# An MoE trunk layer on one core: weights of an expert in one row, in a ring of 24 slabs with two halves

## What is computed

```python
logits = (t @ w_router + b_router)            # 32 experts
top_val, top_idx = lax.top_k(logits, TOP_K)   # 4 for each token
gates = softmax(top_val)
# for each expert e, on the tokens that chose it:
up = xb @ w_up[e] + b_up[e]                   # 1024 -> 2048
glu, lin = up[:, :1024], up[:, 1024:]
glu = minimum(glu, 7.0); lin = clip(lin, -7.0, 7.0)
act = glu * sigmoid(1.702 * glu) * (lin + 1)
y = act @ w_down[e] + b_down[e]               # 1024 -> 1024
```

## Time and profile before

| what | value |
|---|---|
| median of 3 runs | 1153.88 us (1153.6 to 1154.08) |
| profiled execution, span | 1152.1 us |
| PE busy | 1130.9 us (98%) |
| VectorE, ScalarE, GpSimd busy | 358.9, 221.7, 85.2 us |
| read from HBM | 436.18 MB, 379 GB/s over the span |
| DMA queue q1 (the loads) | 89.4% of 16 engines' span |
| granted TensorE clock | 0.997 |

### The profile page before, as it was taken

The page is one execution under the profiler, slowest core; times in us unless marked ns, Lnnn a source line. Parts: engine busy times, 40 slices in busy tenths (PEclk is TensorE's granted clock), DMA queues, the critical chain, the costliest instruction groups (busy, mean ns, idle before and its releaser), DMA issues.

```text
span 1152.1 us, 16029 instructions
## 1 busy us (share of the span) xinstructions
PE 1130.9 (98%) x5376; PEld 502.2 (44%) x5377; DVE 358.9 (31%) x933; ACT 221.7 (19%) x429; POOL 85.2 (7%) x206
## 2 busy tenths in 40 slices
PE   9999999999999999999999999999999999999999
PEld 6785487653333333333333333333333333333333
DVE  6898413232222222222222222222222222222223
ACT  5321213121111121111111111111111111111113
POOL 2990000000000000000000000000000000000000
PEclk9999999999999999999999999999999999999999
DMA  9464336389999999999999999999999999999995
GB/s 364 188 272 176 146 146 282 156 347 429 429 435 431 427 433 433 427 432 433 396 421 437 437 422 433 437 432 423 437 437 424 431 437 433 424 426 429 424 426 244
DMA packets 28821, 437.76 MB, mean 380 GB/s; under 512 B 4017, under 2 KB 4657, under 8 KB 12017
## 3 DMA queue, kind: packets, MB, share of 16 engines
q1 hardware_dynamic: 27920, 436.10, 89.4%
q10 hardware_dynamic: 864, 1.14, 0.3%
HBM read 436.18 MB, written 1.05 MB: 379 GB/s over the span
## 4 chain that ended last, share of the span: by engine, by line
PE 77%; DMA 20%; SPq 1%; ACT 1%; issue 0%; DVE 0%; ACTq 0%; DVEq 0%
PE bank L1813 28%; DMA ring<-in_w_up_dram 20%; PE bank L1858 16%; PE total L1773 4%; PE bank L1760 4%; PE bank L1452 2%; PE bank L1471 2%; PE bank L1866 2%; PE bank L1683 2%; PE bank L1462 2%; PE bank L1767 1%; PE bank L1617 1%; PE total L1617 1%; DMA ring<-in_w_in_dram 1%; PE bank L1911 1%; PE bank L1576 1%
## 5 line engine op out<-in xcount | busy, mean ns | idle before, releaser
L1813 PE MATMUL bank<-ring,buf_m 128*64 128x512 f32 (+1 forms) x2192 | 465.2, 581 | 13.4 <-DMA ring<-in_w_up_dram 13.3
L1813 PEld LDWEIGHTS bank<-ring,buf_m 128*64 128x64 f32 x2192 | 156.9, 138 | 316.1 <-issue 286.4
L1858 PE MATMUL bank<-ring,buf_m 128*64 128x512 f32 x1056 | 239.9, 595 | 0.0
L1343 DVE COPY buf_f<-bank 128x512 f32<-128x512 f32 x32 | 22.1, 692 | 448.6 <-PE bank L1813 448.6
L1858 PEld LDWEIGHTS bank<-ring,buf_m 128*64 128x64 f32 x1056 | 72.8, 136 | 136.5 <-issue 126.5
L888 ACT ACTIVATE buf_m<-buf_f 128x256 f32<-128x256 f32 x32 | 13.3, 416 | 333.1 <-DVE buf_f L1353 333.1
L1773 PE MATMUL total<-buf_m,wr_sb 64*128 64x512 f32 x272 | 67.6, 615 | 1.6 <-ACT buf_m L897 0.8
L656 POOL TENSOR_TENSOR buf_v<-table,buf_v 128x4 f32<-128x4 f32 x33 | 6.6, 201 | 775.6 <-DVE buf_v L1331 775.3
L1760 PE MATMUL bank<-buf_k,buf_v 128*64 128x512 f32 x264 | 63.9, 605 | 0.0
L1349 DVE TENSOR_TENSOR buf_f<-bank,buf_v 128x512 f32<-128x512 f32 x64 | 44.0, 687 | 57.7 <-PE bank L1866 57.7
L897 ACT ACTIVATE buf_m<-bank,buf_v 128x512 f32<-128x512 f32 x32 | 22.0, 687 | 194.1 <-PE bank L1858 194.1
(11 more groups left out here) (389 smaller groups left out, 884.4 us busy)
## 6 DMA issues: line engine op xcount, KB each, us to landing
ring<-in_w_up_dram SPq DMA_DIRECT2D x48, 4096.0 KB, 30.0
ring<-in_w_down_dram SPq DMA_DIRECT2D x24, 4096.0 KB, 30.4
ring<-in_w_up_dram SPq DMA_DIRECT2D x29, 2048.0 KB, 15.3
ring<-in_w_down_dram SPq DMA_DIRECT2D x13, 2048.0 KB, 38.2
ring<-in_w_down_dram SPq DMA_DIRECT2D x6, 1024.0 KB, 10.8
ring<-in_w_up_dram SPq DMA_DIRECT2D x6, 1024.0 KB, 38.5
ring<-in_w_in_dram SPq DMA_DIRECT2D x4, 1024.0 KB, 17.2
ring<-in_w_xkv_dram SPq DMA_DIRECT2D x2, 2048.0 KB, 27.4
```

The lines of the kernel that those rows point to most:

```text
L1813: ins = t_.matmul(banks[bank][h * 64:(h + 1) * 64, c0:c1], xg[:, k, :], w[:, :, k % 4, h, :], start=first, stop=last)
L1858: ins = t_.matmul(banks[2][h * 64:(h + 1) * 64, :], actT[:, f, :], group(slot_of(at))[:, lo + h * BANK:lo + (h + 1) * BANK], start=f == 0, ...
```

## The change

The ring grows to 24 slabs in two halves of twelve; expert e always takes half e % 2. The last two slabs take the place of `buf_v` (slab 22) and `buf_x` (slab 23). w_up and w_down of an expert are joined on the host to one row of twelve slabs per partition (`w_expert`). Experts 4 to 7 are still loaded in three transfers of four slabs, experts 8 to 27 in two of six. The first of them waits for three of the four up groups of expert e-2, the second for the end of its down products. Second, w_xo is loaded in two parts: the second right behind w_out, into slabs 20 and 21, the first behind xq3. The loads that fill the ring first come in another order. g_final goes into slab 0 and is loaded while expert 30 runs, behind all up weights of expert 31 and w_down's first half. Third, small buffers move: the router's constants are written by GpSimd behind xo3, sig and actT lie in U's space. The wait on "late" in VectorE's last section is as before; the diff does not touch it. What PE computes in an expert is the same.

```diff
-RING, LOADS, CYCLE = 20 // GROUP, 12 // GROUP, 5
-TURNS = (E - 2) // CYCLE - 1
-WIDE_FROM, WIDE_TO = 4, 28
+SLABS = 12
+WIDE_FROM, SIX_FROM, SIX_TO = 4, 8, 28
...
-        ring = sb("ring", 20 * SLAB)
+        ring = sb("ring", 2 * SLABS * SLAB)
...
-        wxo_sb = slab(4, 4).rearrange("p (k n) -> p k n", k=KT)
-        buf_x = sb("buf_x", TT * D)
+        wxo_sb = slab(18, 4).rearrange("p (k n) -> p k n", k=KT)
+        buf_v = slab(22)
+        buf_x = slab(23)
...
-        gfin = buf_v[:, 0:D]
+        gfin = slab(0)[:, 0:D]
...
             sp.dma_start(wout_sb, w_out[0].rearrange(kp, p=P)).then_inc(loaded["wout"], 16)
+            w_xo_v = w_xo[0].rearrange(kp, p=P)
+            sp.dma_start(wxo_sb[:, 4:8, :], w_xo_v[:, 4:8, :]).then_inc(loaded["wxo1"], 16)
...
             wait_drained(sp, "w11")
-            sp.dma_start(wxo_sb, w_xo[0].rearrange(kp, p=P)).then_inc(loaded["wxo"], 16)
+            load_up(0, 0, 2)
+            load_up(0, 0, 3)
             wait_drained(sp, "xq3")
-            load_up(1, LOADS, 2)
-            load_up(1, LOADS, 3)
+            sp.dma_start(wxo_sb[:, 0:4, :], w_xo_v[:, 0:4, :]).then_inc(loaded["wxo0"], 16)
+            load_up(1, 1, 2)
...
-            load_up(0, 0, 2)
-            load_up(0, 0, 3)
-            sp.dma_start(gfin, g_final.rearrange("(a n) -> a n", a=1).broadcast_to([P, D])).then_inc(loaded["late"], 16)
-
-            wait_drained(sp, "meta")
+            load_up(1, 1, 3)
+            load_down(1, 1, 0)
+            wait_full(sp, "gT")
+            load_down(1, 1, 1)
...
+            def load_six(e, p, i):
+
+                lo = i * 3 * WIDE
+                sp.dma_start(slab(p * SLABS + i * 6, 6), w_expert[e, :, lo:lo + 3 * WIDE]).then_inc(slabs_in[p][3 * i], 16)
+
+            def load_expert_in_two(e, p):
+
+                n2 = last_block(e - 2)
+                sp.wait_ge(up_steps, n2 * UPS + 3)
+                load_six(e, p, 0)
+                sp.wait_ge(down_steps, n2 * DOWNS + DOWNS)
+                load_six(e, p, 1)
...
             for i in range(DOWNS):
-                sp.wait_ge(up_steps, n2 * UPS + (DOWNS + i + 1))
-                load_up(E - 1, at, i)
+                sp.wait_ge(up_steps, n2 * UPS + (i + 1))
+                load_up(E - 1, 1, i)
+            for q in range(2):
+                for k in range(2):
+                    if q == 0:
+                        sp.wait_ge(up_steps, n2 * UPS + (DOWNS + k + 1))
+                    load_slab(up_v, E - 1, 1, DOWNS + k, DOWNS + k, q, last_up_in[q][k])
+                if q == 0:
+                    sp.wait_ge(down_steps, n2 * DOWNS + 1)
+                    load_down(E - 1, 1, 0)
+            sp.wait_ge(up_steps, n1 * UPS + 1)
+            sp.dma_start(gfin, g_final.rearrange("(a n) -> a n", a=1).broadcast_to([P, D])).then_inc(loaded["late"], 16)
             sp.wait_ge(down_steps, n2 * DOWNS + DOWNS)
...
             for q in range(2):
-                load_slab(down_v, E - 1, at, UPS + 1, 1, q, last_down_in[q])
+                load_slab(down_v, E - 1, 1, UPS + 1, 1, q, last_down_in[q])
```

More of the change, by code:

```diff
@@ L83, in build_program @@
                   b_conv_ln, w_out, g_xattn, g_mem, w_xq, w_xkv, w_xo, g_ffn, w_router, b_router,
-                  w_up, b_up, w_down, b_down, g_final, x_t, mem_t, by_channel, out):
+                  b_up, b_down, g_final, x_t, mem_t, by_channel, w_expert, out):
     fp32, i32, u32 = mybir.dt.float32, mybir.dt.int32, mybir.dt.uint32
@@ L230, in build_program @@
         P2bv = [mean_w[:, 0:P], channel_vecs[:, 0:P]]
-        out_sb = buf_x[:, :].rearrange("p (a n) -> p a n", a=TT)
+        out_sb = slab(2).rearrange("p (a n) -> p a n", a=TT)
         U_sb = buf_f[:, 0:1024]
         A_sb = buf_f[:, 1024:2048].rearrange("p (j h t) -> p j h t", j=KT, h=2)
+        by_column = U_sb.rearrange("p (j s t) -> p j s t", j=KT, s=2)
+        sig = by_column[:, :, 0, :]
+        actT = by_column[:, :, 1, :]
         xg = buf_m[:, 0:512].rearrange("p (k s) -> p k s", k=KT)
[L236 to L239, removed]
+        y_sb = buf_m[:, 512:1024]
         low_banks = [ctx.enter_context(nc.psum_tensor(f"bank{i}", [P, BANK], fp32)) for i in range(4)]
@@ L321, in build_program @@
         gates_ready = sem("gates_ready")
-        first_slabs = sem("first_quarter_slabs_of_first_expert_used")
-        head_in = [sem(f"down_quarter{q}_of_second_expert_in") for q in (0, 2)]
+        router_set = sem("router_constants_set")
         table_ready = sem("ranks_and_gates_in_table")
-        group_in = [sem(f"slabs{i * GROUP}_to_{i * GROUP + GROUP - 1}_in") for i in range(RING)]
+        slabs_in = [[sem(f"half{p}_slabs_from_{i * GROUP}_in") for i in range(UPS + DOWNS)] for p in range(2)]
         p2_ready = sem("onehot_for_gather_ready")
@@ L384, in build_program, with group, starts, transfers_into @@
         kp = "(k p) n -> p k n"
[L385 to L392, removed]
-        WIDE = GROUP * SLAB
+        up_v = w_expert[:, :, 0:UPS * GROUP * SLAB]
+        down_v = w_expert[:, :, UPS * GROUP * SLAB:]
+        def group(p, i):
+            return slab(p * SLABS + i * GROUP, GROUP)
+        WIDE = GROUP * SLAB
+        def starts(e):
+            if SIX_FROM <= e < SIX_TO:
+                return (0, 3)
+            return (0, 2, 4) if WIDE_FROM <= e < SIX_FROM else range(UPS + DOWNS)
+        def transfers_into(e, i):
+            return sum(1 for q in range(e % 2, e + 1, 2) if i in starts(q))
         def krowsq(i):
@@ L481, in last_block, with load_slab @@
                 return sp.snap(first + extra)
-            n1 = last_block(0)
-            def load_second_down(part, half, signal):
+            def load_slab(w, e, p, i, part, half, signal):
                 lo = part * WIDE + half * SLAB
[L489 to L493, removed]
@@ L508, in load_wide, with load_expert @@
[L508 to L513, removed]
+                sp.dma_start(slab(p * SLABS + i * GROUP + half), w[e, :, lo:lo + SLAB]).then_inc(signal, 16)
+            def load_expert(e, p):
+                n2 = last_block(e - 2)
+                for i in range(UPS):
+                    sp.wait_ge(up_steps, n2 * UPS + (i + 1))
+                    if e == E - 2 and i == UPS - 1:
+                        load_slab(up_v, e, p, i, i, 0, late_up_in)
+                        load_slab(up_v, e, p, i, i, 1, slabs_in[p][i])
+                    else:
+                        load_up(e, p, i)
+                for i in range(DOWNS):
+                    sp.wait_ge(down_steps, n2 * DOWNS + (i + 1))
+                    load_down(e, p, i)
@@ L515, in load_expert_wide, with load_four @@
+            def load_four(w, e, p, i, part):
+                lo = part * 2 * WIDE
+                sp.dma_start(slab(p * SLABS + i * 4, 4), w[e, :, lo:lo + 2 * WIDE]).then_inc(slabs_in[p][2 * i], 16)
+            def load_expert_wide(e, p):
                 n2 = last_block(e - 2)
-                sp.wait_ge(up_steps, n2 * UPS + UPS)
-                load_wide(up_v, e, j * LOADS, 0)
+                for i in range(2):
+                    sp.wait_ge(up_steps, n2 * UPS + 2 * (i + 1))
+                    load_four(up_v, e, p, i, i)
@@ L518, in load_expert_wide @@
                 sp.wait_ge(down_steps, n2 * DOWNS + DOWNS)
[L519 to L557, removed]
@@ L559, in _ @@
+            for e in range(2, WIDE_FROM):
+                load_expert(e, e % 2)
+            with sp.Fori(WIDE_FROM // 2, SIX_FROM // 2) as turn:
+                for p in range(2):
+                    load_expert_wide(turn * 2 + p, p)
+            with sp.Fori(SIX_FROM // 2, SIX_TO // 2) as turn:
+                for p in range(2):
+                    load_expert_in_two(turn * 2 + p, p)
+            for e in range(SIX_TO, E - 1):
+                load_expert(e, e % 2)
             n2, n1 = last_block(E - 3), last_block(E - 2)
@@ L636, in _ @@
             wait_drained(pool, "xo3")
+            g.memset(e_base[:, 0:E], 0.0).then_inc(router_set, 1)
+            g.iota(e_row, pattern=[[1, E]], base=0, channel_multiplier=0,
+                   allow_small_or_imprecise_dtypes=True).then_inc(router_set, 1)
+            g.affine_select(out=before[:, :], in_=ones[:, :], compare_op=ALU.is_gt, fill=0.0,
+                            base=0, pattern=[[1, P]], channel_multiplier=-1).then_inc(router_set, 1)
+            g.affine_select(out=sel32[0:E, E:2 * E], in_=ones[0:E, 0:E], compare_op=ALU.is_gt, fill=0.0,
+                            base=0, pattern=[[1, E]], channel_multiplier=-1).then_inc(router_set, 1)
+            g.tensor_copy(sel32[0:E, 0:E], ident[0:E, 0:E]).then_inc(router_set, 1)
+            g.memset(gates2, 0.0).then_inc(router_set, 1)
+            wait_drained(pool, "wo12")
+            g.memset(y_sb, 0.0).then_inc(zeroed, 1)
             g.memset(cap_row[:, 0:TT], float(CAP)).then_inc(cap_set, 1)
             g.memset(cap_row[:, TT:], 0.0).then_inc(cap_set, 1)
-            wait_drained(pool, "wo12")
-            g.memset(y_sb, 0.0).then_inc(zeroed, 1)
```

(45 more changed lines are left out.)

185 lines of the change are left out of this document (66 added, 119 removed).

## The result

The changed kernel takes 1161.38 us (median, 1160.44 to 1162.27), the kernel before, run beside it, 1153.98 us: ratio 1.0067, interval 1.0054 to 1.0080. That is 0.7% slower. Forecast were 1159.5 us and slower. The profiled execution has a span of 1160.6 us.

A forecast was written before the change was run, and what follows sets the result against it. The load queue bounds the kernel; last landing 1132.8 us. But g_final's wait starts the transposes at 1130.0, plus 25.7 tail and 2.0 clock: span 1157.7, 5.6 over before, so 1159.5 us; range 1155.0 to 1164.0.

The forecast's parts named there:

- The last landing: End of the load queue: last weights land at 1132.8 us instead of 1139.1 us.
- Part (d): Coarser loads ask later; queue runs dry around expert 11's second round: 2.2 to 2.3 us lost for 1.9, plus 0.4.
- (a): Load queue before expert 0: two more expert slabs are in before the full stretch begins, minus 4.9 us.
- (b): Load queue, expert 1: down weights come as two transfers instead of four, minus 0.1 us.
- (c): Load queue, experts 8 to 27: two six-slab transfers (14.54 us each) for three of four slabs, minus 1.7 us.
- B: Load queue: six-slab transfers move at the 2 MB pace or worse, about 1166 us or more; chance 0.07, shared with D (request gaps).
- C: Load queue: every transfer costs a constant 2 us, PE becomes the bound, no less than 1134.8 us; chance 0.01.
- g_final: Last expert: its late load lands at 1127.9 us, VectorE's wait holds PE's transposes until 1130.0 us.
- Rival A: Last expert: g_final does not hold up the tail; 1147.6 us with no hold at all; chance 0.12.
- The tail: From the last expert's transposes to the end: 25.7 us as before, plus 2.0 us for low clock after 11 us idle.

The follow-up runs named there:

- experiment 2: Kernel before, with only the load of g_final moved behind all up weights of the last expert: 1166.99 us, ratio 1.0117.
- experiment 6: Four-slab kernel with the wait at first use, one 2 MB load of expert 1 issued behind wo12 instead of behind xq3: 1150.53 us, ratio 0.9973.
- experiment 7: Four-slab kernel with the wait at first use, experts 4 to 27 loaded in six transfers of two slabs each: 1150.67 us, ratio 0.9975.
- experiment 1: Changed kernel (its kernel is kernel 1), VectorE's wait for g_final moved to the first instruction that reads it: 1150.39 us, ratio 0.9972.
- experiment 3: Changed kernel with unused products ahead of PE's wait in the last expert: 1166.83 us with 20 products, 1159.58 us with 10.
- kernel 4: Changed kernel with g_final's wait at first use and experts 8 to 27 loaded in three four-slab transfers: 1145.99 us, ratio 0.9931.
- kernel 5: Changed kernel with g_final's wait at first use and six-slab transfers only from expert 16 on: 1147.88 us, ratio 0.9952.

## Why the prediction was right, and where it was off

**The last landing.** Forecast 1132.8 us, measured 1132.8. That it fits to the tenth is luck: errors cancel. Part (d) was too small: expert 12's second load landed at 572.4 us and not at 576.5, so the queue was dry for longer. The lone transfer issued at 572.0 us took 18.5 us for a length of 14.5 (I had 17.2), and the source view of L525 in that window shows it:

```profile
L525 SPq DMA_DIRECT2D ring<-in_w_expert_dram x1: 333/333/333, 572.0 to 572.0; - x1
...
DMA to landing us min/median/max: 18.5/18.5/18.5
```

The share of that window says how much: 12% of 30 us, 3.6 us, against 5% or 1.5 us in the kernel before. That is 2.1 us where my sum had 0.4. What paid for it: I had carried all delays of the old stream over to the new one. One of them, some 1.5 us in the transfer that lands near 455 us, is in the kernel before and again in experiment 2 at the same place, but not in the changed kernel. And the changed kernel was ahead from the start: its first load of expert 4 lands at 319.9 us for 327.9 before, 8.0 us, of which parts (a), (b) and g_final's own 1.2 us, not yet paid there, explain 6.2. Against these stands one more loss, 1.1 us in a transfer that lands at 1057.6 us. The cause of these three is open. PE did not wait at expert 11, where I had 2.0 us: its up products run there for 13.90 us from 534.64 without a gap.

**Part (a)** is confirmed by experiment 6 (4.5 us for 4.9), **(c)**, as to the price of a transfer, by experiment 7 (0.065 for 0.08 us). The six-slab transfers follow the fit: the chain of waits of the changed kernel has landings at 855.47 + 40.44 and 912.77 + 41.27, four transfers apart.

```profile
855.47 40.44 DMA ring<-in_w_expert_dram
...
912.77 41.27 DMA ring<-in_w_expert_dram
...
1089.58 38.23 DMA ring<-in_g_final_dram
```

(954.04 - 895.91) / 4 = 14.53 us, forecast 14.54. Rivals B and C fall with it. The last row is the term that I named: g_final's transfer stands in the chain that ended last.

**g_final.** Forecast to land at 1127.9 us, landed at 1127.8; transposes forecast for 1130.0, began at 1130.08. The mechanism is shown from both sides: experiment 1 takes the wait away and the loss goes, experiment 2 puts the late load into the kernel before and the loss comes. Rival A, that landings could cross, falls: g_final arrived in its order.

**The tail** is the term that was too small. From the transposes to the last down product 17.6 us (1130.08 to 1144.04 + 3.65) against 14.8 before: 2.8 us lost and 2.0 forecast, 3.1 against the 14.5 of experiment 3. PE was idle for 9.6 us and not 11: it came to the wait at 1120.5, not at 1118.9. The mechanism was as forecast, the size was carried over from a pause of 2.21 us.

The rest of the 2.9 us between the forecast and the profiled span (1157.7, 1160.6) is the output: its two transfers land after

```profile
DMA to landing us min/median/max: 3.4/4.4/5.5
```

in this execution (the source view of L566), against 2.6 and 3.5 us before and 2.7 and 3.6 in all eight variants. That makes 1.9 us. Other executions of the changed kernel had spans of 1158.8 to 1159.2 us, so it is probably an accident of the profiled one. They lie 1.1 to 1.5 us over the forecast, of which the clock makes 0.8 to 1.1.

**The balance of the change**: the longer ring with its order of loads brings some 8 us (kernel 4 against the kernel before, which differ in all but the transfers' size and g_final's wait); six-slab transfers take 2 to 4 us of them back (kernel 1 against kernel 4), 2.5 of them at the experts before 16 (kernel 5), where the late request is; the wait on g_final, with the low clock behind it, takes 11.0 us (changed kernel against kernel 1).

## What to carry to other kernels

When a load moves to the end of a full queue, look for every wait on it, not only at the use: a wait at the head of a section that was free when the load was early holds all that engine's work, and here PE behind it. On a full queue the number of transfers was worth almost nothing here (0.065 us each), and the moment at which they are asked for decided; where a data-dependent stretch frees buffers late, small requests refill sooner (569.2 us for 572.0). And PE's idle time in front of a tail was paid twice, once as idleness (9.6 us) and once as a low clock behind it (3.1 us).

## What was not expected

The price of a pause in clock was not the same twice, and I can't say why: after 9.6 us idle the clock stayed at 0.50 for 6.5 us of work in the changed kernel, and the stretch took 17.6 us. After 11.5 us idle in experiment 2 it stayed there for 3.5 us, and the same work took 16.1:

```profile
1131.20:1137.80 6.60, 0.00 (x0) 0.00 (x0) 0.73 (x4) 0.00 (x0) 0.00 (x0) 0.50 1.02 420
1137.90:1141.40 3.50, 3.50 (x18) 2.92 (x20) 2.52 (x7) 0.75 (x3) 0.20 (x1) 0.50 0.21 89
```

Twenty fp32 products of 128x128 by 128x512 took 17.4 us, 0.87 us each, twice what I had read off a matmul row: the rows count records, and the twenty products are 40 of them. So the 64 up products of an expert, counted off such rows, are 32 products of the program. A buffer of its own for g_final, which would need no late load, was not tried.
